# First modulation in four column pieces, a buffer for each of its weight slices, and the bias table loaded later

## The reference, cut to what matters

```
c_act = silu(c)
mod = (c_act @ ada_w[i] + ada_b[i])[:, None, :]          # 1024 x 6144 weights
sh1, sc1, g1, sh2, sc2, g2 = split(mod, 6)
h = rmsnorm(x, mix_norm_pre[i]) * (1.0 + sc1) + sh1
qkv = h @ w_qkv
...
scores = q k / 8
logits = where(mask, scores + bias[bucket(rel)], -1e30)  # bias from a 32 x 16 table
p = softmax(concat(logits, sink))
```

## Time and profile before

| | us |
|---|---|
| Median of three runs | 2113.91 |
| Lowest and highest of them | 2108.55, 2118.98 |
| Span of the profiled execution | 2109.7 |

### The profile page before, as it was taken

How to read it: one execution, slowest core, us unless ns; L and a number is a source line. 1 busy time by engine, 2 the same in 40 slices (tenths; PEclk the granted TensorE clock), 3 DMA queues, 4 the chain that set the end, 5 groups by cost and what they waited for, 6 DMA issues and landing times.

```text
span 2109.7 us, 22413 instructions
## 1 busy us (share of the span) xinstructions
PE 1777.2 (84%) x7293; PEld 1069.0 (51%) x7293; DVE 1458.9 (69%) x3032; ACT 912.1 (43%) x2383; POOL 618.7 (29%) x573
## 2 busy tenths in 40 slices
PE   4888999899988799997788777988998877777776
PEld 3757998798877454442232232455554422323222
DVE  6676867777776677766676767527677667677675
ACT  2446433534473344444444444424444444444443
POOL 1160000000001344443344333213454433443431
PEclk9988999999999999999999999999999999999999
DMA  9753668555566899999999999967999999999996
GB/s 369 283 200 120 259 224 317 200 200 202 198 220 200 338 421 420 421 421 419 420 421 422 421 421 422 369 219 294 416 418 421 421 421 421 421 421 421 421 422 258
DMA packets 114837, 723.80 MB, mean 343 GB/s; under 512 B 11520, under 2 KB 13360, under 8 KB 34208
## 3 DMA queue, kind: packets, MB, share of 16 engines
q0 software_dynamic: 74864, 540.30, 61.8%
q1 hardware_dynamic: 39856, 182.07, 23.6%
HBM read 721.24 MB, written 1.08 MB: 342 GB/s over the span
## 4 chain that ended last, share of the span: by engine, by line
DMA 38%; PE 33%; DVE 14%; ACT 7%; issue 5%; POOL 3%; SPq 0%; DVEq 0%; ACTq 0%; POOLq 0%
DMA X<-in_k_uv,EI 28%; PE PS L2254 11%; DMA Z<-in_k_uv,EI 8%; PE PS L1943 5%; PE PS L1945 4%; PE PS L1944 4%; DVE junk L1930 3%; PE PS L2230 3%; DVE ACC L1554 3%; POOL X L1067 2%; DVE WL L1570 2%; PE PS L2038 2%; DMA W<-in_ada_w 1%; ACT WH L1076 1%; PE PS L2271 1%
## 5 line engine op out<-in xcount | busy, mean ns | idle before, releaser
L2254 PE MATMUL PS<-X,dg 128*128 128x512 f32 x1380 | 666.5, 615 | 136.8 <-ACT dg L1076 135.3
L1930 DVE CUSTOM_DVE_ANT_0 junk<-H,X 128x1024 f32<-128x1024 f32 x345 | 421.7, 1222 | 245.0 <-DMA X<-in_k_uv,EI 235.0
L1067 POOL DMA_INDIRECT X<-in_k_uv,EI x345 | 371.0, 1075 | 515.7 <-PE PS L2254 324.7
L2254 PEld LDWEIGHTS PS<-X,dg 128*128 128x128 f32 x1380 | 248.6, 193 | 511.8 <-ACT dg L1076 301.8
L1076 ACT ACTIVATE CF<-DOT 128x1 f32<-128x1 f32 x512 | 103.6, 202 | 667.1 <-DVE DOT L1930 664.8
L2254 PE MATMUL PS<-Z,dg 128*128 128x512 f32 x480 | 234.3, 614 | 60.8 <-ACT dg L1076 60.5
L1076 ACT ACTIVATE dg<-CP,CG 128x128 f32<-128x128 f32 x512 | 205.5, 401 | 16.7
L1930 DVE CUSTOM_DVE_ANT_0 junk<-H,Z 128x1024 f32<-128x1024 f32 x120 | 146.7, 1223 | 92.5 <-DMA Z<-in_k_uv,EI 90.2
L2254 PEld LDWEIGHTS PS<-Z,dg 128*128 128x128 f32 x480 | 83.7, 190 | 193.7 <-ACT dg L1076 128.7
L1943 PE MATMUL PS<-XH,WH 128*128 128x256 f32 x592 | 175.8, 297 | 3.8 <-DVE WL L1570 2.2
L1944 PE MATMUL PS<-XL,WH 128*128 128x256 f32 x592 | 170.9, 289 | 0.0
(11 more groups left out here) (320 smaller groups left out, 2574.9 us busy)
## 6 DMA issues: line engine op xcount, KB each, us to landing
W<-in_ada_w SPq DMA_DIRECT2D x56, 1024.0 KB, 5.7
Y<-in_ada_w SPq DMA_DIRECT2D x16, 1024.0 KB, 6.2
W<-in_k_win SPq DMA_DIRECT2D x16, 1024.0 KB, 5.0
W<-in_k_ffi SPq DMA_DIRECT2D x13, 1024.0 KB, 6.2
Y<-in_k_ffi SPq DMA_DIRECT2D x9, 1024.0 KB, 4.9
W<-in_ffn_w_out SPq DMA_DIRECT2D x8, 1024.0 KB, 6.2
W<-in_peer_wq SPq DMA_DIRECT2D x8, 1024.0 KB, 13.2
W<-in_ab_w_out SPq DMA_DIRECT2D x6, 1024.0 KB, 5.2
```

Source lines behind the costliest of these rows:

```text
L1067: e.indirect_dma_start(out=WS[k][:, :], out_offset=None, in_=I[f"k_uv{ly}"][:, :], in_offset=bass.IndirectOffsetOnAxis(ap=EI[t][:, j:j + 1 ...
L1930: e.tensor_tensor_reduce(junk, H[:, t, :], d[:, 0:D], 1.0, 0.0, ALU.mult, ALU.add, DOT[:, j:j + 1]).then_inc(v_dot, 1)
L2254: p = e.matmul(PS[:, 2 * t + q, :], dgb[n % 4][:, :], d[:, D + q * 512:D + (q + 1) * 512], start=(j == 0), stop=(j == 127))
```

## The change

The plan of the first stage is rewritten:

- Slices 5, 6 and 7 are loaded into Z0, Z1 and X0 (`START`). All eight slices of the first modulation thus have a buffer of their own, and SyncE can issue their loads at once. The ring's count starts three places lower for everything behind.
- `ada 7` becomes four steps `adaq q`, each over 512 of 2048 columns: blocks 2q, 2q+1 (shift) and 2q+8, 2q+9 (scale). Behind each stand four products with the column of ones (`modp 0 q q`), in a bank of its own, and for each a step `modq q`: bias and scale of two chunks. `xt` of a chunk waits only for its piece.
- All eight chunks are transposed ahead, two to a PSUM bank.
- The loads of parts 0 and 1 stand together behind slice 7. The first half of part 0 is split before the first chunk and the second half behind chunk 3.
- `bias` and `be` move from behind slice 5 to behind the evacuation of part 0.

```diff
+START = {5: 13, 6: 14, 7: 3}
...
     for c in range(8):
-        if c < 7:
-            P("xp", 0, c, first[c])
-    ada(*range(6))
-    P("bias")
-    P("be")
-    ada(6)
+        P("xp", 0, c, 4 + c % 2 + c // 4 * 2)
+    ada(*range(7))
     P("small2")
-    ada(7)
+    P("lda", 7)
+    for q in range(4):
+        P("adaq", q)
+        P("modp", 0, q, q)
     P("ldw", 0)
+    P("ldw", 1)
     P("split", 0, 0)
-    P("split", 0, 1)
-    mod(0, 3)
-    P("xp", 0, 7, 3)
-    P("ldw", 1)
-    P("g", 1)
     for c in range(8):
-        P("xt", 0, c, first[c])
+        if c % 2 == 0:
+            P("modq", c // 2)
+        P("xt", 0, c, 4 + c % 2 + c // 4 * 2)
         if c:
             P("xl", 0, c - 1)
+        if c == 3:
+            P("split", 0, 1)
     P("xl", 0, 7)
     split(1)
     for n in range(3):
...
         ada(8 + 2 * n)
         gemm(n, n)
         P("evac", n)
+        if n == 0:
+            P("bias")
+            P("be")
         split(n + 2)
         ada(9 + 2 * n)
...
+        elif kind == "lda" and a[0] in START:
+            k = START[a[0]]
...
+                elif kind == "adaq":
+                    q = a[0]
+                    d, arrived, count = slot("lda", 7)
+                    w.wait_ge(arrived, count)
+                    w.wait_ge(v_ada, vada(6))
+                    acc = by_q(ACC)[:, :, q, :]
+                    e.scalar_tensor_tensor(out=acc, in0=by_q(d)[:, :, q, :], scalar=CS[:, 7:8], in1=acc, op0=ALU.mult,
+                                           op1=ALU.add).then_inc(v_ada if q == 3 else v_aq, 1)
+                elif kind == "modq":
...
+                        e.tensor_tensor(m, sums, bias, ALU.add).then_inc(v_own, 1)
+                        w.wait_ge(v_own, own.up())
...
+                    e.scalar_tensor_tensor(out=G1c[:, z], in0=MC[0][:, 8 + 2 * q:10 + 2 * q], scalar=1.0,
+                                           in1=C1[:, c_mp + 2 * q:c_mp + 2 * q + 2], op0=ALU.add,
+                                           op1=ALU.mult).then_inc(v_gq, 1)
...
+                        take(b)
+                        for j in (2 * q, 2 * q + 1, 2 * q + 8, 2 * q + 9):
+                            p = e.matmul(PS[:, b, j:j + 1], src[:, j * 128:(j + 1) * 128], ones[:, 0:1],
+                                         start=True, stop=True)
+                        p.then_inc(p_mod if q == 3 else p_mq, 1)
```

More of the change, by code:

```diff
@@ L102, in row @@
             P("rowa", w, h - 1, b)
-    low, first = (0, 1, 2), (0, 1, 2, 4, 5, 6, 7, 3)
+    low = (0, 1, 2)
     P("init")
@@ L824, in build @@
              "tt", "pq", "rt", "dg", "pi", "band", "grp", "po", "w"))
-        p_x, p_lo = sem("p_x"), sem("p_lo")
+        p_x, p_lo, p_mq = sem("p_x"), sem("p_lo"), sem("p_mq")
+        v_aq, v_gq = sem("v_aq"), sem("v_gq")
         (a_cs, a_sq, a_rt, a_nm, a_hi, a_xtm, a_xth, a_ev, a_ff, a_as, a_at, a_ao, a_rv, a_row, a_lam, a_gsq, a_ds,
@@ L903, in by_k, with by_q @@
             return ap[:, :].rearrange("p (k n) -> p k n", k=k)
+        def by_q(ap):
+            return ap[:, :].rearrange("p (a q n) -> p a q n", a=2, q=4)
         def arena(ly):
@@ L1141, in _ @@
                     z = XT[:, u % 3, :]
+                    o = 256 if i == 0 and c % 4 > 1 else 0
                     if c % 2:
-                        w.wait_ge(p_xt, nth("xp", i, c))
+                        w.wait_ge(p_xt, nth("xp", i, c if i else 7))
                         if i == 4:
@@ L1146, in _ @@
                         else:
-                            w.wait_ge(v_g, 1 if i == 0 else 2) if i < 2 else w.wait_ge(v_s12, i - 1)
+                            if i == 0:
+                                w.wait_ge(v_gq, c // 2 + 1)
+                            elif i == 1:
+                                w.wait_ge(v_g, 1)
+                            else:
+                                w.wait_ge(v_s12, i - 1)
                         if u >= 3:
                             w.wait_ge(v_xtl, u - 2)
-                        act(z, PS[:, b, 0:256], ACT.Identity, scale=scale[:, c:c + 1],
+                        act(z, PS[:, b, o:o + 256], ACT.Identity, scale=scale[:, c:c + 1],
                             bias=bias[:, c:c + 1]).then_inc(a_xtm, 1)
@@ L1555, in _ @@
                                                    op1=ALU.add).then_inc(v_ada, 1)
+                elif kind == "adaq":
[7 more added lines that the diff above has]
+                elif kind == "modq":
+                    q = a[0]
+                    z = slice(2 * q, 2 * q + 2)
+                    m, bias, sums = (x.rearrange("p (a c) -> p a c", a=2)[:, :, z] for x in (
+                        MC[0][:, 0:16], C1[:, c_ab:c_ab + 16], PS[:, q, 0:16]))
+                    if q < 3:
+                        w.wait_ge(p_mq, q + 1)
+                    else:
+                        w.wait_ge(p_mod, 1)
+                    w.wait_ge(v_small, 1)
+                    if q < 3:
+                        e.tensor_tensor(m, sums, bias, ALU.add).then_inc(v_own, 1)
+                        w.wait_ge(v_own, own.up())
+                    else:
+                        e.tensor_tensor(m, sums, bias, ALU.add).then_inc(v_mod, 1)
+                        w.wait_ge(v_mod, 1)
+                    e.scalar_tensor_tensor(out=G1c[:, z], in0=MC[0][:, 8 + 2 * q:10 + 2 * q], scalar=1.0,
+                                           in1=C1[:, c_mp + 2 * q:c_mp + 2 * q + 2], op0=ALU.add,
+                                           op1=ALU.mult).then_inc(v_gq, 1)
                 elif kind == "mod":
@@ L1571, in _ @@
                 elif kind == "g":
[L1572 to L1579, removed]
+                    w.wait_ge(v_mod, 3)
+                    e.scalar_tensor_tensor(out=G2c[:, :], in0=MC[0][:, 32:40], scalar=1.0, in1=C1[:, c_fp:c_fp + 8],
+                                           op0=ALU.add, op1=ALU.mult).then_inc(v_g, 1)
                 elif kind == "s12":
@@ L1587, in _ @@
                     u = nth.use["xt", i, c] - 1
+                    o = 256 if i == 0 and c % 4 > 1 else 0
                     if c % 2 == 0:
-                        w.wait_ge(p_xt, nth("xp", i, c))
+                        w.wait_ge(p_xt, nth("xp", i, c if i else 7))
                         if i == 4:
                             w.wait_ge(g_gn8, 1)
-                        elif i < 2:
-                            w.wait_ge(v_g, i + 1)
+                        elif i == 0:
+                            w.wait_ge(v_gq, c // 2 + 1)
+                        elif i == 1:
+                            w.wait_ge(v_g, 1)
                         else:
@@ L1597, in _ @@
                             w.wait_ge(v_xtl, u - 2)
-                        e.tensor_scalar(XT[:, u % 3, :], PS[:, b, 0:256], scale[:, c:c + 1],
+                        e.tensor_scalar(XT[:, u % 3, :], PS[:, b, o:o + 256], scale[:, c:c + 1],
                                         bias[:, c:c + 1], ALU.mult, ALU.add).then_inc(v_xtm, 1)
@@ L2033, in _ @@
                     w.wait_ge(g_init, 2)
+                    if s == 0:
+                        q = a[2]
+                        if q < 3:
+                            w.wait_ge(v_aq, q + 1)
+                        else:
+                            w.wait_ge(v_ada, vada(7))
+                        take(b)
[3 more added lines that the diff above has]
+                        p.then_inc(p_mod if q == 3 else p_mq, 1)
+                        free[b] = [(v_gq, q + 1)]
+                        continue
                     w.wait_ge(v_ada, vada(8 * MOD_SLICE[s] + 7))
@@ L2057, in _ @@
                         w.wait_ge(v_hs, c // 2 + 1)
-                    take(b)
+                    if i or c % 4 < 2:
+                        take(b)
+                    o = 256 if i == 0 and c % 4 > 1 else 0
                     for t in range(2):
                         x = OB[c // 2 % 2][:, 2 * (c % 2) + t, :] if i == 4 else src[:, t, c * 128:(c + 1) * 128]
-                        p = e.transpose(PS[:, b, t * 128:(t + 1) * 128], x, ident)
+                        p = e.transpose(PS[:, b, o + t * 128:o + (t + 1) * 128], x, ident)
                     p.then_inc(p_xt, 1)
```

## The result

The changed kernel takes 2118.83 us in the median (2115.09 to 2121.1, 8 runs), the kernel before 2112.64 us beside it (8 runs): ratio 1.0025, 95% interval 1.0013 to 1.0037. It is slower by about 5 to 6 us, inside the 0.5% that was called no change; forecast were +4.6 us, 2118.5. The profiled spans are 2116.4 and 2109.7 us, 6.7 apart.

The account below looks back on a forecast made before the run. The start was taken as bound by DMA bytes, the first BE read by VectorE's work and the bytes passing before it. Front +1.45 gained, DMA 6.05 lost, net +4.6 on 2113.9 gave 2118.5 us; range 2107 to 2127.

Parts of the forecast that it names:

- Eight buffers: Slices 5, 6 and 7 issued earlier but arriving as before through a full queue: gain 0, at most 2.46 us.
- Last slice in four: Slice 7 in four pieces: first ends at 32.4, last XL at 46.8 instead of 48.58, gain 1.8 us.
- Table on TensorE and VectorE: Late table's matmuls take 1.2 us after the first projection part; 1.45 us gain left at part 2's split.
- BE issued at 57.9: Table's write begins at 52.7; at 5.2 us from issue to issue, BE's load is issued at 57.9.
- Bytes ahead of the first read: Six loads plus BE, 9.44 MB from 56.8, pass by 80.5; first read taken at 81.9, +4.6 us.
- Front +1.45, DMA -6.05, net +4.6: At the first BE read: 1.45 us gained in front, 6.05 us lost on DMA, net 4.6 us slower.
- No slack behind the read: After the first BE read: no row takes the delay up, so the end moves with the read, +4.6 us.
- 2118.5 on the median: Whole kernel: median of 2113.9 us plus 4.6 gives 2118.5 us.
- The fit of the Trainium skill: DMA before the first read: 2.0 us plus bytes at 436 GB/s, read at 78.5 to 81, sum about +2.5 us.
- Rival A: BE fits into gaps of the six loads, lands before 75 us: -3.5 to -1.5 us, 2110.4 to 2112.4; chance 0.2.
- Rival B: Longer TensorE idle keeps weight matmuls slow through the first four units: +11.6 us, 2125.5; chance 0.1.
- Rival C: Early buffers and pieces do nothing, late table costs nothing: within 1 us of before, 2114; chance 0.1.

Follow-up runs that it names:

- e3: The kernel before with only the three borrowed buffers for slices 5, 6 and 7; 2111.36 us, ratio 0.9994 to the kernel before.
- e2: The kernel before with only the bias table moved behind the evacuation of part 0, no new buffers or pieces; 2120.64 us, ratio 1.0033.
- e1: The changed kernel with only the bias table (sum, write, load of BE) put back behind slice 5; 2111.95 us, ratio 0.9993 to the kernel before.
- e5: e4 with slice 10 in a further free buffer (X5); 2111.98 us, ratio 0.9991 to the kernel before.
- e7: e4 with BE loaded in two halves, the second after the first unit's read; 2110.54 us, ratio 0.9981 to the kernel before.
- e9: e7 with the first attention unit ahead of slice 14 and slice 10 in its own buffer; 2107.44 us, ratio 0.9974 to the kernel before.
- e4: e1 with ScalarE rounding part 0's second half (WH) ahead of the first chunk; 2110.33 us, ratio 0.9988 to the kernel before.

## Why the prediction was right, step by step

- **Eight buffers, 0.** Right. Slice 6 landed at 28.47 (28.4 forecast), and e3 changed nothing.
- **Last slice in four, sums from 32.4, last XL at 46.8.** Right: 32.7 and 46.45; the wait for ScalarE's half, 1.42 us, stands where it was put.
- **Table on TensorE and VectorE; 1.45 us of gain left at part 2's split.** 1.26, with errors that partly cancel. The first part was to end 3.65 us after the last XL, as before; it took 4.53 (46.45 to 50.98), because TensorE's matmuls turned from 0.41 to 0.28 us no earlier (at 48.6; 48.1 before) though the work began earlier. Against that stand the last XL, 0.35 earlier than forecast, and the table's matmuls, 0.97 us on the chain instead of 1.2.
- **BE issued at 57.9.** Wrong by 2.9 us. The table's write landed in 1.8 us and not in 4.9, beside emptier queues (DMA share 0.47 in 53 to 54 us, 0.13 in 54 to 55). It did not help: q0 moved 2 packets of BE before 60 us, and BE landed 28.1 us after its issue.
- **Bytes ahead of the first read, 9.44 MB, through at 80.5.** Right: in 56 to 80 us the two queues moved 6.32 and 3.08 MB, 9.40 together. What was too small is what follows the bytes. Slice 14 was used at 81.70 and BE landed at 83.1, where the sum had the landing at 80.5; the read came at 83.97, where 81.9 was taken and 83.1 was the upper of the two cases. The kernel before shows the same lag: its queue had moved the 6.29 MB of the six loads by 73.3 us and slice 14 was used at 74.99. The forecast's 374 GB/s, taken from issue to landing, had this lag in it, and its end of the range, +7, is what the read did (+6.7); the 393 to 402 GB/s of the stretches had not. Whether the lag is the slowest of the sixteen engines or the time from the last byte to the signal, the runs don't tell.
- **Front +1.45, DMA -6.05, net +4.6.** The net at the read is +6.7; if 1.3 is taken as gained, 8.0 were lost. But the gain at part 2's split is not a gain at the read. By the runs, the late table alone costs 7.4 there (e2), and the new front gives 0.2 under the early table (e1) and 0.7 under the late one (e2 to the changed kernel, 84.69 to 83.97).
- **No slack behind the read.** Right as to direction. In the two profiles the distance from first to last read of BE is 67.6 us after and 67.7 before, and the end moved by 6.7; that these agree so well is luck. In e1 the first read is 0.2 us earlier than before and the last 2.1 later (147.1 to 145.0), with the same time by the ratio.
- **2118.5 on the median.** Measured were 2118.83, and part of this hit is luck: the forecast started from 2113.9, the median of three runs, where the kernel before took 2112.64 beside the changed one. The difference was 6.2 in the medians and 5.3 by the ratio, for 4.6 forecast.
- **The fit of the Trainium skill, "DMA: Bandwidth & Descriptors", section "Anatomy of one DMA" (2.0 us plus bytes at 436 GB/s).** As the prediction's estimate from that page, it put the read at 78.5 to 81; measured were 83.97. The engines gave 400 to 407 GB/s with both queues on, so the rows of before were the better guide.
- **Rival A, the gain stays.** Fell: BE landed at 83, not before 75. **Rival B, slow TensorE.** Fell as a price: the weight matmuls are slow after the first read again (0.42 us at 86.32), fast from 89.5 on, although TensorE's idle time ahead of the first unit had grown from 3.50 to 7.32 us. **Rival C.** The half of it on buffers held, the half on the table fell with e1 and e2.

The pieces' own worth remains open in part. e1 has pieces and early table, e3 neither pieces nor late table, and their times are the same (0.9993 and 0.9994). In e1's profile part 0 is evacuated only 0.24 us before, as TensorE's matmuls stayed at 0.41 us until 50.4 there (until 48.6 in the changed kernel's profile). Whether that is the pieces' doing or the chance of one profile was not tried. No run has the pieces without the buffers.

## What to carry to other kernels

A load that looks early and idle may be filling a stretch in which the other loads wait for buffers; before moving it, look at their column in the stretch it leaves and in the one it enters, and add up the bytes that must pass before the next bound read, and the lag from the last byte to the use. Where both buffers and bytes are near the limit, one alone gives little (e5 0.6 us at the second unit, e7 1.4); together with the new order (e9) the second unit came at 77.73 instead of 80.35 in e4, which is about the sum of the steps, and their times can't be told apart by the intervals. Count a front's gain at the wait that ends last behind it, not where the work was shortened (e4: 3.3 us there, 1.4 at the read).

## What the runs showed of the hardware

- A small write of 32 KB to device memory landed in 1.8 us where the DMA share was 0.47 and then 0.13 (changed kernel, 53 to 55 us), and in 4.9 us behind full queues (kernel before, share 1.00 in 29 to 34 us).
- The 3 MB load with rows of 1536 bytes moved its first packets 4 to 4.5 us after its issue (34.46 to 38.5 before, 55.03 to 59.5 after).
- The same load needed 21.4 us in one place and 28.1 us in another, at the same packet-for-packet trade (70 to 69, 74 to 72) with the 1 MB loads. Before, the other queue ran dry at about 50 us and the load had the engines to itself in 50 to 52 (371 GB/s); after, the other queue was never empty.
- A 1 MB load that VectorE stood waiting for was used 1.7 us after its queue had moved all bytes up to its last (slice 14: 73.3 to 74.99 before, 80.0 to 81.70 after).
- Matmul rate and granted clock don't always agree in one row: in the kernel before, the stretch 42 to 46 us shows 1.00, in e1 0.50, and both have matmuls of 0.41 us there, 0.21 us from start to start.
